# Starting the stores of the k products and of the convolution rows from SyncE instead of ScalarE

## The reference

```python
proj = h @ w_in                              # h: (1056, 1024)
qkv, z, a, b, u, gate_a, gate_b = jnp.split(proj, cuts, axis=-1)
qkv, conv_new = _causal_conv(qkv, conv_buf, conv_w)   # 4 taps, then silu
q, k, v = jnp.split(qkv, 3, axis=-1)         # 8 heads of 64 each
q, k = _l2norm(q), _l2norm(k)
...                                          # chunks of 64 tokens
a_mat = where(strict, einsum('bhncd,bhnsd->bhncs', kb, k) * decay, 0)
sol = triangular_solve(a_mat + eye, rhs)     # unit lower triangular
```

## Time and profile before

| | |
|---|---|
| median of 3 runs | 1656.95 us |
| the runs | 1653.67 to 1658.68 us |
| profiled execution, its own time | 1655.12 us |
| its span | 1653.3 us |
| mean granted clock of TensorE | 0.97 of 2.4 GHz |
| instructions | 16293 |
| HBM read and written | 188.83 and 83.24 MB |

### The profile page before, as it was taken

How to read it: one execution, slowest core, us unless ns; L and a number is a source line. 1 busy time by engine, 2 the same in 40 slices (tenths; PEclk the granted TensorE clock), 3 DMA queues, 4 the chain that set the end, 5 groups by cost and what they waited for, 6 DMA issues and landing times.

```text
span 1653.3 us, 16293 instructions
## 1 busy us (share of the span) xinstructions
PE 1531.5 (93%) x6131; PEld 954.5 (58%) x6131; DVE 735.6 (44%) x1311; ACT 398.9 (24%) x662; POOL 200.6 (12%) x224
## 2 busy tenths in 40 slices
PE   8999999989987989999989999999939999999975
PEld 6676666645655656556989766555414444444432
DVE  4667776022342433798577443245433221121116
ACT  3211101015466664331313220001111111111113
POOL 0000010000000000154368200000110000000004
PEclk9998999999999999999989999999959999999998
DMA  5263883423231012316221425232387999999948
GB/s 164 79 110 119 246 245 85 133 91 80 78 91 39 15 40 90 87 56 166 75 71 29 144 70 180 62 116 111 122 300 279 366 372 367 364 375 368 365 149 314
DMA packets 232261, 273.25 MB, mean 165 GB/s; under 512 B 62516, under 2 KB 167336, under 8 KB 231920
## 3 DMA queue, kind: packets, MB, share of 16 engines
q1 hardware_dynamic: 204628, 203.54, 39.7%
q10 hardware_dynamic: 18140, 34.48, 5.5%
q0 software_dynamic: 9408, 34.08, 5.2%
HBM read 188.83 MB, written 83.24 MB: 165 GB/s over the span
## 4 chain that ended last, share of the span: by engine, by line
PE 77%; DVE 7%; ACT 6%; issue 4%; POOL 2%; DMA 2%; ACTq 0%; POOLq 0%; SPq 0%; DVEq 0%
PE P L694 24%; PE P L1143 12%; PE P L1094 7%; PE P L1050 7%; PE P L1127 6%; PE P L851 2%; PE P L875 2%; PE P L1114 2%; POOL arena L602 1%; DVE arena L1449 1%; PE P L720 1%; PE P L826 1%; POOL arena L661 1%; DVE arena L1451 1%; PE P L1074 1%
## 5 line engine op out<-in xcount | busy, mean ns | idle before, releaser
L694 PE MATMUL P<-arena 128*128 128x352 f32 (+1 forms) x1728 | 538.5, 467 | 7.8 <-ACT arena L2133 6.5
L694 PEld LDWEIGHTS P<-arena 128*128 128x128 f32 (+1 forms) x1728 | 325.2, 192 | 195.4 <-issue 38.0
L1143 PE MATMUL P<-arena 128*128 128x512 f32 x512 | 227.1, 597 | 0.8 <-ACT arena L2234 0.8
L1143 PEld LDWEIGHTS P<-arena 128*128 128x128 f32 x512 | 95.6, 192 | 109.6 <-issue 109.6
L1094 PE MATMUL P<-arena 128*128 128x512 f32 (+1 forms) x288 | 128.9, 597 | 1.9 <-DVEq L1627 1.9
L1771 DVE COPY arena<-P 128x512 f32<-128x512 f32 x32 | 22.1, 692 | 220.5 <-PE P L1114 220.5
L1127 PE MATMUL P<-arena 128*128 128x512 f32 x256 | 115.3, 593 | 0.9 <-DVE arena L1811 0.9
L1050 PE MATMUL P<-arena 128*128 128x352 f32 x384 | 115.1, 459 | 0.8 <-DMA arena<-y_d 0.8
L1050 PEld LDWEIGHTS P<-arena 128*128 128x128 f32 x384 | 72.9, 190 | 41.3 <-issue 0.8
L602 POOL TENSOR_TENSOR arena<-arena,N 64x256 f32<-64x256 f32 x96 | 81.1, 845 | 49.8 <-ACT arena L2155 28.4
L1094 PEld LDWEIGHTS P<-arena 128*128 128x128 f32 (+1 forms) x288 | 50.2, 181 | 62.3 <-issue 59.8
(11 more groups left out here) (405 smaller groups left out, 1894.2 us busy)
## 6 DMA issues: line engine op xcount, KB each, us to landing
arena<-in_w_expert_up_dram SPq DMA_DIRECT2D x32, 2048.0 KB, 13.4
arena<-in_w_expert_down_dram SPq DMA_DIRECT2D x32, 1024.0 KB, 7.4
arena<-in_w_in_dram SPq DMA_DIRECT2D x36, 512.0 KB, 4.1
x_d<-zero SPq DMA_DIRECT2D x4, 4096.0 KB, 20.1
arena<-x_d POOLq DMA_DIRECT2D x32, 512.0 KB, 5.9
y_d<-arena ACTq DMA_DIRECT2D x32, 512.0 KB, 7.8
gate_d<-arena ACTq DMA_DIRECT2D x16, 528.0 KB, 4.8
arena<-gate_d SPq DMA_DIRECT2D x24, 352.0 KB, 3.1
```

The costliest lines, as they stand in the source:

```text
L694: m = pe.matmul(P[0:p, b + j, 0:TBK], w[:, k, 0:p], hT[:, k, TBK * j:TBK * j + TBK], start=f, stop=l)
L1143: m = pe.matmul(P[:, i % 2, :], xgT[i % 2][:, k, :], WU[i % NWE][:, k, :], start=k == 0, stop=k == KD - 1)
```

## The change

ScalarE keeps the reads of bank 7 into the stage buffer. Where it started the two stores of the k products and the two of the convolution rows, it now only keeps account of them (`hand_over`): which buffer, and which count of `s_7f` says that the read is done. SyncE starts the same stores, from the same buffers, into the same destinations and onto the same semaphores, in `staged_rows(n)`, after waiting for that count. It calls `staged_rows(n - 2)` after `weights(n)`, and so ahead of the clear that follows that load and ahead of `weights(n + 1)`. The rows of steps 18 to 26 are stored in the first loop, those of steps 27 and 28 after the loads for jobs 29 and 30, ahead of the wait for `s_kk` and the load of `TP`; those of step 29 after the load for job 31. The store of the sample rows stays on ScalarE.

```diff
--- before.py
+++ after.py
@@ -522,7 +522,7 @@
 
         X_PARTS, Z_PARTS = 4, 8
         EARLY = NWE
-        sent = {}
+        sent, staged = {}, {}
         block = ctx.enter_context(nc.Block())
 
         @block.gpsimd
@@ -1876,6 +1876,14 @@
                 pending[b].append((sems[b], sent[sems[b]]))
                 nstg[0] += 1
 
+            def hand_over(sems, copies, m):
+
+                b = nstg[0] % 2
+                sent[sems[b]] = sent.get(sems[b], 0) + 16 * copies
+                pending[b].append((sems[b], sent[sems[b]]))
+                staged[sems is s_kk, m] = b, n7[0]
+                nstg[0] += 1
+
             def spill(dst, width):
                 send(s_stg, (dst, stage[nstg[0] % 2][:, 0:width]))
 
@@ -2116,16 +2124,13 @@
                     o = stage_free()
                     for q in range(2):
                         read7(act.activation(o[:, 512 * q:512 * q + 512], bank7(), ACT.Copy))
-                    ov = o[:, 0:SEQ].rearrange("p (c j) -> p c j", j=C)
-                    send(s_kk, *[(kk_d[hp, h].rearrange("c i j -> i c j"), ov[64 * h:64 * h + 64]) for h in range(2)])
+                    hand_over(s_kk, 2, m)
                 m = n - 1
                 if post1(m):
                     bk = bank7()
                     o = stage_free()
                     read7(act.activation(o[0:3 + 3 * NB, 0:128], bk[0:3 + 3 * NB, 0:128], ACT.Copy))
-                    f = f_tile(m)
-                    send(s_cvo, (conv_p[0, 0][:, 128 * f:128 * f + 128], o[0:3, 0:128]),
-                         (conv_s[0].rearrange("n i f -> (n i) f")[:, 128 * f:128 * f + 128], o[3:3 + 3 * NB, 0:128]))
+                    hand_over(s_cvo, 2, m)
                     if JOBS[m][0] != "v":
 
                         act.wait_ge(s_ss, QK_COUNT(m))
@@ -2349,8 +2354,27 @@
                 sp.dma_start(op[0, 0].rearrange("(a b) p -> a (b p)", b=2), FINO[0:GA, 2 + d, :]).then_inc(s_out, 16)
 
 
+            def staged_rows(n):
+                m = n - 2
+                if post1(m) and JOBS[m][0] == "k":
+                    b, read = staged[True, m]
+                    sp.wait_ge(s_7f, read)
+                    o = stage[b][:, 0:SEQ].rearrange("p (c j) -> p c j", j=C)
+                    for h in range(2):
+                        sp.dma_start(kk_d[JOBS[m][1], h].rearrange("c i j -> i c j"), o[64 * h:64 * h + 64]
+                                     ).then_inc(s_kk[b], 16)
+                m = n - 1
+                if post1(m):
+                    b, read = staged[False, m]
+                    f = f_tile(m)
+                    sp.wait_ge(s_7f, read)
+                    sp.dma_start(conv_p[0, 0][:, 128 * f:128 * f + 128], stage[b][0:3, 0:128]).then_inc(s_cvo[b], 16)
+                    sp.dma_start(conv_s[0].rearrange("n i f -> (n i) f")[:, 128 * f:128 * f + 128],
+                                 stage[b][3:3 + 3 * NB, 0:128]).then_inc(s_cvo[b], 16)
+
             for n in range(N_JOBS_S5, N_JOBS_QKV):
                 weights(n)
+                staged_rows(n - 2)
                 if n == AB:
                     sp.dma_start(abp[:, 0:1], a_log.rearrange("a h -> h a")).then_inc(s_abp, 16)
                     sp.dma_start(abp[:, 1:2], dt_bias.rearrange("a h -> h a")).then_inc(s_abp, 16)
@@ -2372,10 +2396,12 @@
                     sp.dma_start(gcP[:, 1, :], beta_d.rearrange("h (c i) -> (h c) i", i=C)).then_inc(s_gcd, 16)
             for n in range(N_JOBS_QKV, N_JOBS_QKV + 2):
                 weights(n)
+                staged_rows(n - 2)
             for sm in s_kk:
                 sp.wait_ge(sm, sent[sm])
             sp.dma_start(TP.rearrange("p i j -> p (i j)"), kk_d.rearrange("a b c i j -> (a b c) (i j)")).then_inc(s_tp, 16)
             weights(N_JOBS_QKV + 2)
+            staged_rows(N_JOBS_QKV)
 
 
             for sm in s_qsd:
```

## The result

The change makes the kernel slower: a median of 1660.45 us in 20 runs against 1656.86 us in 20 runs of the kernel before, a ratio of 1.0028 with an interval of [1.0020, 1.0036]. That is 3.6 us lost where about 8 were forecast as gained (1648.7 us), and it lies outside the range. The profiled execution took 1658.29 us (span 1656.5), 3.2 us more than the one before.

What follows compares the result with a forecast made beforehand. TensorE, busy 93% of the span, was taken as the bound, waiting on ScalarE's Ln in two steps. Direct 3.9 plus clock 3.5 us, rounded to 7.3, gave 1648.7 us, range 1644 to 1656.5.

Steps and rivals of the forecast that it cites:

- the table load of 1.28 us ends at 533.19: ScalarE, step 23: without the four issues the load follows the copy of line 2125, so the Ln starts 1.95 us earlier.
- the direct part: ScalarE's four DMA issues before the Ln in steps 23 and 25: removing them gains 1.95 and 1.94 us, 3.9 in all.
- All other moved stores: nothing: Stores outside steps 23 and 25 hide behind TensorE's work or sums of squares, so moving them gains nothing.
- The clock behind the two idle times: TensorE's 30 matmul instructions after each shortened wait before line 694 return to full speed: 3.5 us gained, bounds 0 and 3.5.
- The sum, 7.3 us: Direct part 3.9 plus clock part 3.5 gives 7.4 us gained, rounded to 7.3 for small waits.
- SyncE and TP: SyncE starts the moved stores within its waits for jobs, and the later load of TP still lands in time: no cost.
- 6 us of slack: TP, issued later behind the third v tile's stores, lands at 659.7; VectorE wants it at 665.65.
- Rival 1: Idle time shrinks but the clock still drops, or VectorE takes up the faster matmuls: gain 3.9 us only; chance 0.21.
- Rival 2: Nothing arrives: another wait ends at the same time, or fast 2.4 us gaps turn slow; gain 0 to 3 us; chance 0.14.
- Rival 3: Slower: TP lands after 665.65, so VectorE's line 1442 and TensorE's line 867 wait; 24 us landing gives 1660; chance 0.06.

Runs made afterwards that it cites:

- e1: The changed kernel, but in q and k tiles ScalarE no longer waits for its own read of the convolution rows; 1648.88 us, ratio 0.9956.
- e5: The changed kernel with both waits kept and a one-column Ln put ahead of the wait for the sums of squares; 1649.32 us, ratio 0.9952.
- e7: e1 with the load of TP put right behind the weights for job 30, ahead of the third v tile's stores; 1649.46 us, ratio 0.9954.
- e8: The kernel before with four matmuls of unread result on TensorE behind the sums of squares in steps 23 and 25; 1656.90 us, ratio 0.9994.
- e2: The kernel before, no store moved, with one already met wait for bank 7 added at the wait for the sums of squares; 1660.51 us, ratio 1.0023.
- e9: e1 with the sample rows' stores also begun by SyncE and ScalarE's wait for its sample read dropped in q tiles; 1648.49 us, ratio 0.9949.
- e11: The kernel before with unread matmuls on TensorE in every wait of 2.4 us or more of the stage; 1646.44 us, ratio 0.9949.

## Why the prediction was wrong

**The step that failed** is the sentence "the table load of 1.28 us ends at 533.19", and with it the working of the direct part. It put the load right behind the read because that is where it stood. It could stand there only because a DMA issue between the read and the Ln carried the read's wait, and that DMA is what the change removes. In step 23 of the kernel after the load ran from 533.86 to 535.14, 1.95 us later than forecast, and the Ln began at 535.15 instead of 533.37. In the trace of before the load was free in each step, and nothing in a row says why it was. The question that wasn't asked was which instruction will carry the wait of `read7` once nothing lies between it and the Ln.

**"All other moved stores: nothing"** fell with it. The prediction looked at the steps whose second tile is k or v, saw that their issues hide behind the sums of squares, and bounded the price of losing that cover. But there the load itself had been the thing hidden. ScalarE at the table load and the Ln of such a step, after and before:

```profile
553.74 1.28 ACT L2138 ACT_TABLE_LOAD   x1 [2.02 <-PE P L908]
555.04 1.14 ACT L2138 ACTIVATE arena<-P,cst 128x1056 f32<-128x1056 f32 x1
```

```profile
552.53 1.28 ACT L2133 ACT_TABLE_LOAD   x1 [0.65 <-ACT arena L2125]
553.85 1.14 ACT L2133 ACTIVATE arena<-P,cst 128x1056 f32<-128x1056 f32 x1
```

The Ln starts 1.19 us later though its input is there 0.15 us earlier. What follows on ScalarE moves with it, down to the copy of line 2083 for which TensorE's line 860 waits: 2.19 − 0.98 = 1.21 us, three times. With 0.89 at 479.76 and 0.08 at the first line 860 that makes 4.6 us lost; 3.28 − 2.66 = 0.62 us, twice, is gained. The sum is +3.4, the table's direct part is +3.1, the medians differ by 3.6.

**The other steps, by the runs.**
- Direct part, 3.9 us once the load is free: right. −4.1, −4.2 and −4.4 us in e1, e5 and e7; idle time 1.32 us for a forecast 1.3.
- The clock behind the two idle times, 3.5 us: right in e1, e5 and e7 (9.11 us for 30, twice; −3.4 us), where the idle time did fall to 1.3 or 1.4 us. In after it fell to 2.66 and the clock stayed low twice. Counting it per idle time was wrong as a method: e8 shortened the same two by filling them and had nothing of it.
- The sum, 7.3 us: what e1 measured, −7.3 with an interval of about −10 to −4. The size was right for a kernel that the change is not.
- SyncE and TP: right. "6 us of slack" was 6.3, and e7 shows that TP could move by 11.8 us without effect. No weight load was waited for.
- Rival 1 has TensorE's clock stay low, as it did, but with the idle time at 1.3 us. Rival 2 names the fast waits of 2.4 us turning slow, seen in e8. Rival 3, the only slower one, was about TP, which had no part. No rival was about ScalarE's own order, where the cause lay. A slower outcome had 0.07.

The page of the Trainium skill that the prediction weighed, "DMA: Bandwidth & Descriptors", section "Issuing engines are not separate DMA queues", says that moving an issue saves only the sequencer's time. The runs agree in the size where the load is free: 2.45 us of issues gave 1.95 a step, twice. It says nothing of what else an issue does in a stream, which here decided the sign.

## What to carry to other kernels

Before you take an instruction out of a stream, ask which waits it carries. Where two waits fall to one activation with a new table, one of them can become an instruction of its own ahead of the table load, and a 1.28 us load that was hidden then starts only when that wait is met, here in eight places. Compare the built instruction lists of the two kernels, with what each instruction waits for, before you work out any time; if a load is held, drop a wait that is not needed or pull the load ahead with a small activation of the same function. And count what the clock gives over a whole stage, after every long wait in it, not wait by wait.

## What the runs showed of the hardware

- The granted clock behind a wait does not follow from the length of that wait alone. Waits of 2.4 us before line 908 were followed by 2.04 us for six matmul instructions in some places and by up to 3.73 in others, and a wait of 3.33 us was followed by 10.75 us for 30 at 533.98 and by 9.11, full speed, at 586.46 in the same execution of e2. In e9 four waits of 2.03 us were followed by 2.04 us three times and by 3.74 once (at 591.23). After the shortened waits before line 694, 0.9 to 1.8 us in steps 23 and 25, none of the kernels shown ran slow.
- The time at 1.2 GHz in this stretch of 277 us was anything from 0 to 20.5 us, and filling waits with matmuls whose results are not read was worth more (8.4 us, e11) than the whole change was to bring.
- Starting a DMA costs SyncE about what it costs ScalarE: in step 23 the two k stores took 1.33 us (0.62 and 0.69 on ScalarE) and the two convolution stores 0.69 and 0.71 us (0.33 and 0.72 on ScalarE); behind the third v tile the latter took 0.24 and 0.30.
